# A hybrid decoder trunk on one core: attention and inverse segments weighted a third more in the list that spreads them over expert ticks

## What is computed

```python
def reference(x, c, ...):
    c_act = jax.nn.silu(c)
    for l in range(DEPTH):                     # DEPTH = 2
        mod = c_act @ ada_w[l] + ada_b[l]
        sh_m, sc_m, g_m, sh_f, sc_f, g_f = jnp.split(mod, 6, axis=-1)
        h = _rmsnorm(x, norm_mix_g[l]) * (1.0 + sc_m[:, None]) + sh_m[:, None]
        cols = h @ w_in[l]
        y_a = diff_attention(cols[..., :DIFF_COLS], ...)           # 6 heads
        y_b = rwkv7_time_mix(cols[..., DIFF_COLS:...], ...)        # 6 heads, recurrent
        y_c = forgetting_attention(cols[..., ...:], fox_bf[l])     # 4 heads
        mix = jnp.concatenate([y_a, y_b, y_c], axis=-1) @ w_out[l]
        x = x + g_m[:, None] * mix
        h = _rmsnorm(x, norm_ffn_g[l]) * (1.0 + sc_f[:, None]) + sh_f[:, None]
        x = x + g_f[:, None] * peer_ffn(h, peer_wq[l], peer_subkeys[l], peer_u[l], peer_v[l])
    return _rmsnorm(x, final_norm_g)
```

## Time and profile before

| | |
|---|---|
| median of 3 runs | 1893.32 us (1893.13 to 1895.14) |
| the profiled execution, its own time | 1892.43 us |
| its span in the profile | 1890.6 us |
| mean granted clock of TensorE | 0.947 of full speed |
| mixing of tile 0 and modulation, before the first tick | about 286 us |
| three phases with mixing beside (from tick 0 to the next tick 0) | 428.8, 420.9, 425.7 us |
| last phase, without mixing | 313.2 us |

### The profile page before, as it was taken

How to read it: one execution, slowest core, us unless ns; L and a number is a source line. 1 busy time by engine, 2 the same in 40 slices (tenths; PEclk the granted TensorE clock), 3 DMA queues, 4 the chain that set the end, 5 groups by cost and what they waited for, 6 DMA issues and landing times.

```text
span 1890.6 us, 20925 instructions
## 1 busy us (share of the span) xinstructions
PE 1616.0 (85%) x6868; PEld 1005.9 (53%) x6868; DVE 1394.5 (74%) x3315; ACT 665.3 (35%) x1634; POOL 515.2 (27%) x564
## 2 busy tenths in 40 slices
PE   2767689898999998898999989899999987887776
PEld 2656575554665655564656655555655653332222
DVE  5877598978765748988765748979775749985554
ACT  1313125426632235336633135426632133231112
POOL 2110022222233232222233232222233233333331
PEclk9879799999999999999999999999999998999999
DMA  9994669998899999998999999998899999999996
GB/s 396 422 380 165 244 263 420 376 384 301 292 401 421 420 421 399 364 415 312 332 407 422 420 420 396 368 398 296 303 405 421 421 397 400 411 409 421 422 422 253
DMA packets 96989, 706.08 MB, mean 373 GB/s; under 512 B 10992, under 2 KB 11504, under 8 KB 13296
## 3 DMA queue, kind: packets, MB, share of 16 engines
q0 software_dynamic: 80640, 587.24, 77.5%
q1 hardware_dynamic: 16240, 117.50, 15.2%
HBM read 703.64 MB, written 1.05 MB: 373 GB/s over the span
## 4 chain that ended last, share of the span: by engine, by line
PE 48%; DVE 30%; DMA 16%; issue 3%; ACT 3%; POOL 0%; DVEq 0%; ACTq 0%; POOLq 0%
PE psum L775 27%; DMA ringmem<-in_peer_uv_dram,eidx 10%; DVE ringmem L1440 9%; PE psum L651 5%; DMA ringmem<-in_ada_pairs_dram 3%; DMA W<-in_w_groups_dram 3%; PE psum L415 2%; PE psum L638 2%; DVE ringmem L1084 2%; PE psum L523 1%; PE psum L511 1%; PE psum L418 1%; PE psum L521 1%; DVE coef L1453 1%; ACT diag L1055 1%
## 5 line engine op out<-in xcount | busy, mean ns | idle before, releaser
L775 PE MATMUL psum<-ringmem,diag 128*128 128x512 f32 x2048 | 978.0, 623 | 132.4 <-ACT diag L1055 132.1
L382 POOL DMA_INDIRECT ringmem<-in_peer_uv_dram,eidx x512 | 489.5, 956 | 1139.0 <-PE psum L775 1081.9
L1440 DVE SCALAR_TENSOR_TENSOR ringmem<-ringmem,psum 128x1024 f32<-128x1024 f32 x512 | 612.2, 1220 | 199.2 <-DMA ringmem<-in_peer_uv_dram,eidx 184.0
L775 PEld LDWEIGHTS psum<-ringmem,diag 128*128 128x128 f32 x2048 | 389.2, 199 | 607.7 <-issue 410.3
L1055 ACT ACTIVATE diag<-K,coef 128x128 f32<-128x128 f32 x512 | 176.4, 393 | 223.3 <-DVE coef L1453 223.3
L415 PE MATMUL psum<-hT,W 128*128 128x128 f32 x1344 | 172.5, 287 | 36.8 <-DMA W<-in_w_groups_dram 18.6
L415 PEld LDWEIGHTS psum<-hT,W 128*128 128x128 f32 x1344 | 169.5, 203 | 60.8 <-issue 20.6
L1047 ACT ACTIVATE coef<-dots 128x2 f32<-128x2 f32 x256 | 51.8, 202 | 394.2 <-DVE ringmem L1440 393.3
L1084 DVE SCALAR_TENSOR_TENSOR ringmem<-ringmem,diag 128x1024 f32<-128x1024 f32 x96 | 115.5, 1223 | 23.7 <-DMA ringmem<-in_ada_pairs_dram 21.5
L651 PEld LDWEIGHTS psum<-hT,W 128*128 128x128 f32 x1024 | 121.0, 194 | 12.9 <-issue 7.4
L651 PE MATMUL psum<-hT,W 128*128 128x128 f32 x1024 | 123.8, 277 | 3.5 <-ACT hT L824 3.5
(11 more groups left out here) (243 smaller groups left out, 1608.3 us busy)
## 6 DMA issues: line engine op xcount, KB each, us to landing
ringmem<-in_ada_pairs_dram POOLq DMA_DIRECT2D x48, 1024.0 KB, 20.2
W<-in_w_pieces_dram SPq DMA_DIRECT2D x48, 1024.0 KB, 9.1
W<-in_w_groups_dram SPq DMA_DIRECT2D x24, 1536.0 KB, 11.2
W<-in_w_groups_dram SPq DMA_DIRECT2D x12, 1024.0 KB, 9.6
ringmem<-in_peer_uv_dram,eidx POOLq DMA_INDIRECT x512, 11.8
W<-in_w_groups_dram SPq DMA_DIRECT2D x4, 1040.0 KB, 9.2
attn<-in_subkeys_t_dram SPq DMA_DIRECT2D x4, 1024.0 KB, 9.7
K<-in_consts_dram SPq DMA_DIRECT2D x1, 1546.0 KB, 18.0
```

The lines of the kernel that those rows point to most:

```text
L382: nc.gpsimd.indirect_dma_start(slot(k), None, rows, bass.IndirectOffsetOnAxis(ap=eidx[:, ph % 2, m:m + 1], axis=0)).then_inc(row_landed[q ...
L775: mm = nc.tensor.matmul(acc[:, q], diag[:, k % DIAGS, :], slot(k)[:, D:][:, q], start=(k % SEL == 0), stop=(k % SEL == SEL - 1), skip_grou ...
L1440: ins = v.scalar_tensor_tensor(out=u, in0=u, scalar=1.0, in1=hrep, op0=ALU.mult, op1=ALU.mult, accum_out=dots[:, j:j + 1])
```

## The change

Twenty entries of `COST`, those of segments 29 to 48, are replaced. They rise from 552 to 770 in sum (segment 45 from 30 to 36, most from 32 to 45); the other 59 stay. The sum of all goes from 1783 to 2001. Nothing else changes.

```diff
 COST = [8, 20, 25, 17, 17, 17, 30, 24, 17, 24, 17, 17, 20, 20, 20, 26, 26, 26, 22, 17, 20, 19, 19, 14, 17, 17, 17, 17, 18,
-        28, 30, 30, 28, 32, 32, 32, 32, 32, 32, 32, 32, 32, 28, 28, 25, 30, 18, 22, 22, 35, 34, 34, 34, 34, 34, 28, 28, 20,
+        38, 42, 42, 42, 45, 45, 45, 45, 45, 45, 45, 45, 45, 42, 40, 32, 36, 24, 26, 26, 35, 34, 34, 34, 34, 34, 28, 28, 20,
         17, 21, 17, 21, 17, 21, 17, 21, 17, 21, 17, 21, 17, 21, 17, 21, 10, 14, 14, 10, 5]
```

## The result

The changed kernel takes **1915.72 us** (median of 4 runs, 1912.93 to 1922.72) against 1894.23 us for the kernel before on the same chips: ratio 1.0118, interval 1.0091 to 1.0145. It is slower by 1.2%, three times what was forecast (0.4%), and lies outside the range (1882 to 1911). The profiled execution took 1917.2 us.

A forecast was written before the change was run, and what follows sets the result against it. No engine alone was taken as the bound: VectorE, TensorE or transfers bind by stretch. Terms -6.8 + 18.2 - 8.7 gave +2.7 us a phase, +8.1 for three, on 1892.4: 1900 us, range 1882 to 1911.

The forecast's parts named there:

- B, +18.2 a phase: Segments 29 to 48, four ticks more: 7.1 us with the retrieval parts plus 11.1 for three plain ticks.
- the 15 that was named as a sign of being wrong: Segments 29 to 48: growth of 15 us or less would show the forecast wrong.
- VectorE was to be busy over 90% in ticks 18 to 23: Sign in the changed profile, ticks beside segments 29 to 33: VectorE over 90% busy.
- A, -6.8: Segments 0 to 28, two ticks fewer: 8.8 us saved less 2 for new neighbours, from -10.0 to -3.4.
- The two ticks: Removed from segments 7 to 16 (5.1 us, VectorE's) and 17 to 22 (3.7, TensorE's): 8.8 us saved.
- The penalty for new neighbours: Segments 0 to 28: waits from newly shared ticks cost 2 us, bounds 0 and 4.
- dq's load would be late near tick 9: Segment 15: TensorE would idle for weight group dq, whose load needs 11.2 us and follows segment 12.
- C, -8.7: Segments 49 to 78, two ticks fewer: 5.0 and 3.7 us saved, from -10.0 to -7.4.
- the bare tick at the full 5.0: Tick 45, among segments 49 to 56: removing it saves the full transfer price, 5.0 us.
- The first (transfers pay): Outside segments 29 to 48 only DMA binds: -5.2 us a phase, 1877 us at the end; chance 0.29.
- the second rival: Every stretch bound by computation, work only moved: +0.7 us a phase, 2 us in all, 1893; chance 0.23.
- The third, denser segments stall: Segments 0 to 28 give -3.4, 29 to 48 +20.0, 49 to 78 -7.4: +9.2 us a phase, 1920; chance 0.1.

The follow-up runs named there:

- b_two: Kernel before with two bare ticks moved from the end of the phase to before segments 35 and 42: 1894.50 us, ratio 0.9993.
- a_only: Kernel before with only segments 0 to 28 placed as in the changed kernel, the two saved ticks bare at the phase's end: 1916.45 us, ratio 1.0105.
- a_regroup: Changed kernel with the same ticks per stretch but other segments sharing ticks among segments 7 to 22: 1904.15 us, ratio 1.0044.
- part_both: Changed kernel with segment 8 moved from tick 5 to 6 and segment 15 from tick 9 to 10: 1900.62 us, ratio 1.0025.
- a_1011: a_regroup with segments 10 and 11 in tick 7, 12 and 13 in tick 8, 14 alone in tick 9: 1901.64 us, ratio 1.0032.
- part_78: Changed kernel with segment 8 alone moved from tick 5 to tick 6: 1916.05 us, ratio 1.0096.
- part_15: Changed kernel with segment 15 alone moved from tick 9 to tick 10: 1907.75 us, ratio 1.0074.
- a_78: a_regroup with segments 7 and 8 together in tick 5 and 9 alone in tick 6: 1913.02 us, ratio 1.0096.
- c_only: Kernel before with only segments 49 to 78 placed as in the changed kernel, the two saved ticks bare at the phase's end: 1894.91 us, ratio 0.9996.

## Why the prediction was wrong, point by point

*B, +18.2 a phase*: right by the cuts on TensorE, +17.8. By the forecast's own cuts it is 15.5 in the mean, and in the third phase, at 13.8, under the 15 that was named as a sign of being wrong; the difference turns up in A, -1.4 in the mean by those cuts. So that B comes out to 0.4 us is in part the choice of the cut. In the windows of its bare ticks 21, 25, 29, 33 and 37 (first phase) the last four take 3 us or little more, as said, and tick 21, which has a retrieval part, 4.38:

```profile
441.42:445.80 4.38, 3.78 (x7) 1.79 (x8) 4.17 (x14) 3.16 (x8) 0.44 (x1) 0.71 0.97 337
470.67:474.08 3.41, 3.41 (x22) 2.45 (x21) 2.59 (x6) 3.35 (x10) 1.87 (x2) 1.00 0.38 84
496.12:499.01 2.89, 2.89 (x16) 1.93 (x15) 2.59 (x5) 2.67 (x6) 1.20 (x2) 1.00 0.72 218
521.67:524.68 3.01, 3.01 (x15) 1.81 (x14) 2.59 (x6) 2.94 (x7) 1.44 (x2) 1.00 0.78 261
543.41:546.30 2.89, 2.89 (x11) 1.46 (x10) 2.58 (x5) 0.91 (x4) 0.94 (x1) 1.00 0.84 266
```

The terms are less good than their sum: four ticks at b_two's 3.3 and the retrieval parts at a_only's 2.1 make 15.3, and 2.5 us are unaccounted for. VectorE was to be busy over 90% in ticks 18 to 23. From 19 to 23 it is, 36.79 of 38.96 us, where the earlier trace rows has 29.52 of 31.54; with tick 18, in which it idles, it is 86%:

```profile
426.35:465.31 38.96, 33.20 (x96) 15.63 (x96) 36.79 (x93) 13.46 (x32) 11.30 (x12) 0.91 0.83 312
```

*A, -6.8*: measured -4.2. Both terms of the sum were mis-sized, in opposite ways. The two ticks are worth 9 to 11 us where the two waits are gone (a_regroup -9.3, part_both -10.4, a_1011 -11.5), not 8.8. That this is near the 10.0 of their transfers does not show that transfers bind A: part_both's A moves 397 GB/s, not 421. The penalty for new neighbours was put at 2 with an upper bound of 4, by the nearest row, fk's wait of 3.65. The step that failed is that bound: I listed the waits (7 with 8, 14 with 15, dq's load) and took one wait's length for all of them, where 7 with 8 costs 1.3 to 3.4 (changed kernel over part_78 1.3, part_15 over part_both 2.7, a_78 over a_regroup 3.4), dq's load 3.4 to 4.9 (changed kernel over part_15, part_78 over part_both), and the two together 6.2 (changed kernel over part_both). That dq's load would be late near tick 9 was foreseen and seen; its price was guessed from the length of a wait, and the wait is not all of it. The 3.03 us of idle time are followed by sixteen multiplications that take 1.67 us more than at full clock, 4.7 together. The row of fk, from which the bound was taken, had this already: 3.78 us for sixteen multiplications behind its 3.65 us.

*C, -8.7*: measured -4.8, the largest miss of the three. The step that failed is "the bare tick at the full 5.0": the price of transfers was taken because TensorE showed 3.7 idle us there, and C was called bound by transfers because VectorE waits 31.7 us for rows. The output products show that the bare tick gave 3.4 us, its weighing on TensorE, in c_only and after the change alike (27.7 to 24.3). The tick among the queries gave 2.0 = 3.44 - 2 x 0.72; the new pairs there were not priced at all. VectorE's waits for rows are 28.5 us in the shorter C: they are idle time of an engine with time to spare, and did not say what a removed tick would give. Whether transfers bind C and the end taken together is not shown: c_only's unchanged phases fit it, but its two ticks at the end cost 7.3 us, near TensorE's 6.9.

*The rivals.* The first (transfers pay) had nearly the right size for A once the stalls are out, and the wrong one for B. With the stalls gone the change costs 5.7 us (part_both), between the second rival's 2 and the forecast's 8. The third, denser segments stall, is nearest in the sum, +9.2 a phase worked out and +8.3 measured, and right in what it says of A (-3.4, measured -4.2). In part that is luck: it had B at 20.0 for 17.8 and C at -7.4 for -4.8. It had a chance of 0.1, and the end of the range lay at half of it. The Trainium skill (Perfetto Trace Analysis, Identifying Performance Opportunities, Optimization Strategy) says that interleaving the regimes of a kernel may improve its time. It did not here: B took more time on the bound engine than A and C gave back, even without the stalls (part_both, 1.0025).

*Left open*: the 2.5 us of B; the 1.7 to 3.8 us by which the gap between output product and query grows or shrinks with the ticks ahead of it; and why dq's load takes 8.7 us in the third phase after the change, against 10.5 and 10.1 in the others and 10.6 in a_only's third, so that it is less late there (1.20 us against 3.03 and 2.58).

## What to carry to other kernels

Work that is spread by hand over the steps of another loop has two prices: how many steps a stretch gets, and which pieces fall into one step. Before a list of costs is changed, write out the new neighbours and look for a result that crosses engines within one step, or a buffer that is freed and awaited one step apart: here two such places cost 15 of 21 us, and the number of steps 6. Try such places each alone and together: here one alone gave nothing that the times show, the other 8 us, both 15. And read what follows a wait as well as the wait: the instructions behind it can run at a lower granted clock.

## What was not expected of the hardware

A stretch can show the highest transfer rate of the kernel (421 GB/s), 26 waits of one engine for transfers, and yet give back a removed step at another engine's price (3.44 us, not 5.0). And TensorE waiting 5.3 us for a late coefficient cost nothing in a_1011, while 2.8 us of VectorE in tick 5 cost 1.3 to 3.4: how long an engine idles in one place says little of what the place costs. Behind 3.03 us of TensorE's idle time its clock was at half for 3.4 us; behind 1.20 us in the same place it stayed at full.
